# Identity products in the norms' waits, the output projection among retention's last sums, first values turned late

## Chip, cores and metric
One core of one Trainium2 chip. The metric is device microseconds of one execution; times of the kernel before are a median of three runs, and the profile is of a further execution.

## What is computed
Two layers on 512 latent tokens of width 1024 (and 256 context tokens). Layer 0 mixes with windowed attention beside retention, layer 1 with a Hyena long convolution; each layer has a half-step SwiGLU block before and after its mixer.

```python
def swiglu(h, w_gate, w_up, w_down):
    return (jax.nn.silu(h @ w_gate) * (h @ w_up)) @ w_down

def adaln_in(x, g, m, i):
    return rmsnorm(x, g) * (1.0 + m[:, :, 3 * i + 1]) + m[:, :, 3 * i]

def adaln_out(x, y, g, m, i, w):
    return x + w * m[:, :, 3 * i + 2] * rmsnorm(y, g)

# even layer: y = concat(window_attention, retention_out(o, g)) @ w_out
def retention_out(o, g):
    o = o * lax.rsqrt(jnp.mean(o * o, -1, keepdims=True) + EPS)
    return o.reshape(o.shape[0], o.shape[1], -1).astype(g.dtype) * jax.nn.silu(g)

# odd layer: y = (x0 * bidir_fftconv(v * x1)) @ w_out
```

All of it is float32; the kernel reaches that by splitting activations and weights into a high and a low part and adding three products.

## The kernel before
Activations lie with features on the partitions: eight tiles of 128 features by 512 tokens (256 for context). A weight block is 128 output features by 1024 inputs. SyncE loads it into one of four slots of `raw`; ScalarE copies it to `w_hi` (`split_hi`, L1159), VectorE writes the rest to `w_lo` (`split_lo`, L1698), and TensorE does `three` (L530) for each of its eight input tiles: 24 matmuls of 128x512 a block. Slots come round by the semaphores `lo_split` and `block_done`; results go to PSUM banks 0 to 3 in turn and are given back by `result_read`. Every engine has its program written out by hand in its own order, so an instruction that waits holds up all behind it on its engine.

**Fused norm.** Behind the output projection, two FFNs and the Hyena projection, the norm of the result and that of the next input are made together. `down` or `project` calls `early_sums` before the last six matmuls: three groups of four one-column sums (`stat`, L669), each two passes. `fused_norm` on TensorE (from L680) then waits for the last tile's square, sums it, sums `cross` and `gained`, waits for the reciprocal root (`norm_spread`, L718: four products of 128 columns with the identity), and again for `wide2` (L696, four more). VectorE makes x and `prod` tile by tile, ScalarE `h_hi`, VectorE `h_lo` (L1915), and the next gate/up or Hyena input takes four weight blocks side by side as the tiles come. In the order of time they are called A after the even mixer's projection, B and C after FFNs, and D after Hyena's projection.

**Mixer.** `mixer_second` goes through slots: `score`, a projection in parts (0 to 3, 3 to 6, 6 to 8 input tiles) with the turns of earlier probabilities between, then the probabilities times values. In slot 0 the first values are turned (L802) after part 0 to 3, once VectorE has copied them. `retention` ends with `sums(3)` (L1000) and `spread(3)` (L1006), each waiting for the other engines; `project` follows with eight blocks. Its inputs are attention tiles 0 to 3 and retention tiles 4 to 7, of which the last needs spread(3). In `project` VectorE does for each block: copy y (L2499), add the square, three gain sums, split a weight block two ahead; block 7 has two splits ahead of its copy.

**Hyena's end.** After the back transforms (L1107, L1110) TensorE waits until the gated tiles and the first projection weights are split.

Of the kernel before, what the change touches and what calls it, by code (L numbers as in the profile page):

```python
# [23 lines left out]
P = 128  # L24
# [125 lines left out]
def build(nc, io):  # L150
# [38 lines left out]
    with ExitStack() as ctx:  # L189
# [334 lines left out]
        def _(pe):  # L524
# [108 lines left out]
            def down(s, T, tiles, beside=lambda i: None, bank_of_sums=None):  # L633
# [4 lines left out]
                def step(i, last):  # L638
                    for dd in range(2):
# [4 lines left out]
                        for half in range(2):  # L644
# [3 lines left out]
                            d = 2 * i + dd  # L648
                            if bank_of_sums and half and d:
                                pe.wait_ge(square_ready, n0 + d)  # L650
                                stat(square[:, 1 - dd, :], T, d == 1, False, bank_of_sums).then_inc(square_used, 1)
                            for t in range(per):
                                f = half * per + t
                                if dd == 0 and (f == 0 or f == tiles - 1):

                                    pe.wait_ge(act_ready, f0 + (tiles - 1 if f == 0 else tiles))
                                if s.following and last and j == 3 and t == 3:
                                    early_sums(s)
                                ins = three(psum[:, bank, 0:T], (slot, t * P), P, act_hi[:, f, 0:T], act_lo[:, f, 0:T],
                                            f == 0, f == tiles - 1)  # L660
# [11 lines left out]

            def early_sums(s):

                sum2, sum3, _, _ = gain_buffers(s)
                pe.wait_ge(square_used, KT * at["norm"] + KT - 1)
                stat(sumsq, SEQ, True, False, STAT)
                pe.wait_ge(gain_sums, GAIN_OPS * at["fused"] + GAIN_OPS - 1)
                stat(sum2, SEQ, True, False, GAIN_STAT)
                stat(sum3, SEQ, False, False, GAIN_STAT, 4)  # L680

            def fused_norm(s):


                n, f = at["norm"], at["fused"]
                _, _, cross, gained = gain_buffers(s)
                pe.wait_ge(square_ready, KT * n + KT)
                stat(square[:, 1, :], SEQ, False, True, STAT).then_inc(square_used, 1)
                pe.wait_ge(gain_sums, GAIN_OPS * f + GAIN_OPS)
                stat(cross, SEQ, False, False, GAIN_STAT)  # L690
                pe.wait_ge(gained_ready, KT * f + KT)
                stat(gained[1], SEQ, False, True, GAIN_STAT, 4).then_inc(gain_summed, 1)
                norm_spread(SEQ)
                pe.wait_ge(wide2_ready, f + 1)
                for t in range(SEQ // P):
                    ins = pe.matmul(psum[:, RBC2, t * P:t * P + P], wide2[:, t, :], ident[:, :], start=True, stop=True)  # L696
                ins.then_inc(rbc2_ready, 1)
                at["fused"] += 1

# [27 lines left out]
            def ffn(ss, T):  # L727
# [5 lines left out]
                if ss[3].following:  # L733
                    fused_norm(ss[3])
                else:
                    norm(T, 1)

            def first_ffns():
# [11 lines left out]
                gate_up(sx[0], SEQ, ctx_norm, lambda: pe.wait_ge(filt_ready, PARTS))  # L750
                down(sx[1], SEQ, HALF_TILES[0])
                gate_up(sx[2], SEQ)
                down(sx[3], SEQ, HALF_TILES[1])
# [118 lines left out]
            def mixer_second():  # L872
# [37 lines left out]
                for s in range(len(SLOTS)):  # L910
                    if s >= 1:
                        score(s - 1)
                    proj(s, 0, 3)
                    if s == 0:
                        pe.wait_ge(v_copied, 1)
                        value_turn(lambda t: sumsq[:, t * P:t * P + P], 6, 4)
                        value_turn(lambda t: prod[:, 1, t * P:t * P + P], 7, 2).then_inc(v_turned, 1)
                    else:
                        if s >= 2:
                            turn(s - 2, 0)  # L920
                    proj(s, 3, 6)
                    if s >= 2:
                        turn(s - 2, 1)
                    proj(s, 6, KT)
                    if s >= 1:
# [4 lines left out]
            def retention():  # L930
# [107 lines left out]
                outputs(3)  # L1038
                spread(2)
                sums(3)  # L1040
                spread(3)

            def project(s, ready):

                for d in range(s.blocks):
                    b = s.first + d
                    pe.wait_ge(lo_split, RING + b + 1)
                    pe.wait_ge(result_read, at["p"] + 1)
                    for k in range(KT):
                        if d == 0:  # L1050
                            ready(k)
                        if d == KT - 1 and k == 6:
                            early_sums(s)
                        ins = three(psum[:, at["p"] % 4, :], (b % RING, k * P), P, h_hi[:, k, :], h_lo[:, k, :],
                                    k == 0, k == KT - 1)
# [5 lines left out]
            retention()  # L1061
            project(mix_out, lambda k: pe.wait_ge(att_out_ready, k + 1) if k < 4 else pe.wait_ge(ret_out_ready, k - 3))
            fused_norm(mix_out)
# [79 lines left out]
            pe.wait_ge(g_ready, KT // 2)  # L1143
            project(hy_out, lambda k: pe.wait_ge(g_split, k + 1))
            fused_norm(hy_out)
# [1638 lines left out]
```

## Time and profile before

| | |
|---|---|
| median of three runs | 2457.37 us (2457.02 to 2461.73) |
| the profiled execution | 2460.91 us |
| its span | 2459.2 us |
| TensorE busy | 2351.5 us, 96% |
| VectorE / ScalarE busy | 1368.3 us, 56% / 876.6 us, 36% |
| mean granted TensorE clock | 0.967 |
| DMA | 133 GB/s on average |

Busy shares are of the span. A matmul's time in a row is from its start to its modelled end; back to back they overlap, so prices are read from start to start. The clock of a stretch is the share of full speed that was granted.

### The profile page before, as it was taken

The page shows a single profiled execution, that of the slowest core. Times are in us where ns is not written, and L with a number is a line of the kernel's source. Part 1 is how long each engine was busy: PE and PEld are TensorE (multiplying, and loading weights), DVE is VectorE, ACT ScalarE, POOL GpSimd, SP SyncE. Part 2 cuts the span into 40 slices and gives each one's busy share as a digit, 9 for nine tenths or more (in the row PEclk, how much of TensorE's full clock was granted, in tenths as well). Part 3 has the DMA queues.
Part 4 walks back from the last instruction along what each step waited for, and adds up shares of the span by engine and source line. Part 5 has one row for each costly group of instructions (what it writes and reads, how often), then busy time and mean ns, then how long its engine had stood idle before and what let it go on. Part 6 is the DMA issues. An engine that isn't in the chain of part 4 may idle for free. (4 is left out here: it accounts for less than half of the span.)

```text
span 2459.2 us, 31552 instructions
## 1 busy us (share of the span) xinstructions
PE 2351.5 (96%) x11692; PEld 1933.6 (79%) x11692; DVE 1368.3 (56%) x2020; ACT 876.6 (36%) x1305; POOL 126.1 (5%) x245
## 2 busy tenths in 40 slices
PE   6999999999999988999999999999999989999997
PEld 2588788899987866788888788888877777888886
DVE  5677833575666564733367743743674587433334
ACT  1443122454544573433222432222354214322222
POOL 1022200000021000000011000200000000000000
PEclk8999999999999998899999899999999988999998
DMA  8578932345542101232367322842322212223222
GB/s 334 210 272 296 334 103 71 122 155 195 169 141 76 46 27 35 84 114 86 115 245 257 101 86 90 285 155 75 114 78 78 103 60 77 86 90 106 96 77 77
DMA packets 97104, 327.03 MB, mean 133 GB/s; under 512 B 12288, under 2 KB 12704, under 8 KB 95200
## 3 DMA queue, kind: packets, MB, share of 16 engines
q1 hardware_dynamic: 67968, 222.27, 26.6%
q0 software_dynamic: 28016, 101.99, 12.0%
q8 instruction: 73, 1.20, 0.2%
q10 hardware_dynamic: 1008, 1.25, 0.1%
q14 instruction: 39, 0.32, 0.0%
HBM read 313.67 MB, written 8.39 MB: 131 GB/s over the span
## 5 line engine op out<-in xcount | busy, mean ns | idle before, releaser
L533 PE MATMUL psum<-h_hi,w_hi 128*128 128x512 f32 (+1 forms) x2256 | 857.4, 380 | 28.9 <-DVE h_lo L1915 13.3
L534 PE MATMUL psum<-h_lo,w_hi 128*128 128x512 f32 (+1 forms) x2256 | 848.7, 376 | 0.0
L535 PE MATMUL psum<-h_hi,w_lo 128*128 128x512 f32 (+1 forms) x2256 | 848.2, 376 | 0.0
L1698 DVE TENSOR_TENSOR w_lo<-raw,w_hi 128x1024 fp32r<-128x1024 f32 (+2 forms) x442 | 470.8, 1101 | 87.7 <-ACT w_hi L1159 84.9
L533 PEld LDWEIGHTS psum<-h_hi,w_hi 128*128 128x128 f32 x2256 | 430.4, 191 | 112.4 <-issue 26.5
L1159 ACT ACTIVATE w_hi<-raw 128x1024 fp32r<-128x1024 f32 (+2 forms) x442 | 406.3, 951 | 245.5 <-PE psum L535 160.4
L535 PEld LDWEIGHTS psum<-h_hi,w_lo 128*128 128x128 f32 x2256 | 430.0, 191 | 77.0
L534 PEld LDWEIGHTS psum<-h_lo,w_hi 128*128 128x128 f32 x2256 | 430.6, 191 | 74.2 <-issue 0.7
L533 PE MATMUL psum<-act_hi,w_hi 128*128 128x512 f32 (+1 forms) x880 | 326.4, 371 | 4.9 <-DVE w_lo L1698 4.4
L535 PE MATMUL psum<-act_hi,w_lo 128*128 128x512 f32 (+1 forms) x880 | 324.7, 369 | 0.0
L534 PE MATMUL psum<-act_lo,w_hi 128*128 128x512 f32 (+1 forms) x880 | 324.6, 369 | 0.0
L1831 DVE TENSOR_TENSOR prod<-psum,square 128x512 f32<-128x512 f32 (+1 forms) x110 | 70.1, 638 | 432.5 <-PE psum L535 411.9
L1192 ACT ACTIVATE act_hi<-prod 128x512 f32 (+3 forms) x110 | 64.8, 589 | 506.2 <-DVE prod L1831 506.2
L533 PEld LDWEIGHTS psum<-act_hi,w_hi 128*128 128x128 f32 x880 | 166.6, 189 | 35.3 <-issue 6.3
L535 PEld LDWEIGHTS psum<-act_hi,w_lo 128*128 128x128 f32 x880 | 166.7, 189 | 27.7
L534 PEld LDWEIGHTS psum<-act_lo,w_hi 128*128 128x128 f32 x880 | 166.8, 190 | 27.1
L1732 DVE SCALAR_TENSOR_TENSOR mod_raw<-mod_raw,c_row 128x1024 f32<-128x1024 f32 x128 | 149.7, 1222 | 11.8 <-DMA mod_raw<-in_w_rows 10.4
L1190 ACT ACTIVATE square<-psum 128x512 f32<-128x512 f32 (+1 forms) x110 | 60.6, 551 | 191.9 <-PE psum L535 191.8
L2593 POOL DMA_DIRECT2D mod_raw<-in_w_rows x152 | 80.2, 528 | 804.6 <-DVE mod_raw L1732 718.3
L1836 DVE TENSOR_TENSOR act_lo<-prod,act_hi 128x512 f32 (+3 forms) x110 | 70.3, 639 | 91.1 <-ACT act_hi L1192 91.1
L1942 DVE COPY y<-psum 128x512 f32<-128x512 f32 (+3 forms) x40 | 25.5, 637 | 107.9 <-PE psum L535 107.8
L1245 ACT ACTIVATE square<-y 128x512 f32<-128x512 f32 (+2 forms) x40 | 23.4, 586 | 136.0 <-DVE y L1944 136.0
(298 smaller groups left out, 1778.4 us busy)
## 6 DMA issues: line engine op xcount, KB each, us to landing
raw<-in_gate_up SPq DMA_DIRECT2D x220, 512.0 KB, 4.2
mod_raw<-in_w_rows POOLq DMA_DIRECT2D x152, 512.0 KB, 5.5
raw<-in_down_a SPq DMA_DIRECT2D x80, 384.0 KB, 3.7
raw<-in_down_b SPq DMA_DIRECT2D x80, 320.0 KB, 3.1
raw<-in_hy_in SPq DMA_DIRECT2D x24, 512.0 KB, 3.4
raw<-in_mix_in SPq DMA_DIRECT2D x22, 512.0 KB, 4.1
mod_raw<-in_w_mod POOLq DMA_DIRECT2D x16, 512.0 KB, 7.1
filt_dram<-made SPq DMA_DIRECT2D x6, 1024.0 KB, 4.0
```

What stands on the lines that cost most here:

```text
L533: pe.matmul(out, w_hi[:, slot, c:c + P], hi, start=start, stop=False)
L534: pe.matmul(out, w_hi[:, slot, c:c + P], lo, start=False, stop=False)
L535: return pe.matmul(out, w_lo[:, slot, c:c + P], hi, start=False, stop=stop)
L1159: act.activation(w_hi[:, slot, 0:cols], raw[:, slot, 0:cols], ACT.Copy).then_inc(hi_split, 1)
L1190: act.activation(silu[:, j, 0:T], psum[:, bank, 0:T], ACT.Silu).then_inc(silu_ready, 1)
L1192: act.activation(act_hi[:, bass.ds(2 * i + j, 1), 0:T], prod[:, j:j + 1, 0:T], ACT.Copy).then_inc(act_hi_ready, 1)
L1698: ins = dve.tensor_tensor(w_lo[:, slot, 0:cols], raw[:, slot, 0:cols], w_hi[:, slot, 0:cols].bitcast(F32), ALU.subtract)
L1732: dve.scalar_tensor_tensor(src, src, 1.0, row, ALU.mult, ALU.mult, accum_out=mod_cols[:, k:k + 1]).then_inc(mod_used, 1)
L1831: ins = dve.tensor_tensor(prod[:, j, 0:T], psum[:, bank, 0:T], silu[:, j, 0:T], ALU.mult)
L1836: dve.tensor_tensor(act_lo[:, fl, 0:T], prod[:, j:j + 1, 0:T], act_hi[:, fl, 0:T].bitcast(F32), ALU.subtract).then_inc(act_ready, 1)
L1942: dve.tensor_copy(dst, src).then_inc(result_read, 1)
L2593: pool.dma_start(mod_raw[:, k % RING, :], src).then_inc(mod_landed[k % RING], 16)
```

## The change
A helper `keep_busy(n)` issues n products of the identity with itself (128 columns, into the PSUM bank that comes next) and waits at most for that bank to be read. It is called in all fused norms (3, 2, 1, 6 and 13 products), before the last norm (5), before the second gate/up of the first FFN (8), before the last square's sums of the context FFN (8) and before Hyena's output projection (13). `early_sums` is cut into three groups, before input tile 6, before 7, and after the last matmul. In slot 0 the values are turned after all input tiles. The first two blocks of the output projection are done in `retention`: six tiles of block 0 after spread(2), two of block 1 after sums(3), the rest after spread(3).

```diff
@@ down
                             if bank_of_sums and half and d:
+                                if d == KT - 1:
+                                    keep_busy(8)
                                 pe.wait_ge(square_ready, n0 + d)
...
-                                if s.following and last and j == 3 and t == 3:
-                                    early_sums(s)
+                                if s.following and last and j == 3 and t >= 3:
+                                    early_sums(s, t - 3)
@@
+            def keep_busy(n):
+
+                pe.wait_ge(result_read, at["p"] + 1)
+                for _ in range(n):
+                    pe.matmul(psum[:, at["p"] % 4, 0:P], ident[:, :], ident[:, :], start=True, stop=True)
+
+            def early_sums(s, part):
 
                 sum2, sum3, _, _ = gain_buffers(s)
+                if part == 0:
+                    pe.wait_ge(square_used, KT * at["norm"] + KT - 1)
+                    stat(sumsq, SEQ, True, False, STAT)
+                elif part == 1:
+                    pe.wait_ge(gain_sums, GAIN_OPS * at["fused"] + GAIN_OPS - 1)
+                    stat(sum2, SEQ, True, False, GAIN_STAT)
+                else:
+                    stat(sum3, SEQ, False, False, GAIN_STAT, 4)
@@ fused_norm
+                early_sums(s, 2)
+                keep_busy(3)
                 pe.wait_ge(square_ready, KT * n + KT)
                 stat(square[:, 1, :], SEQ, False, True, STAT).then_inc(square_used, 1)
+                keep_busy(2)
                 pe.wait_ge(gain_sums, GAIN_OPS * f + GAIN_OPS)
                 stat(cross, SEQ, False, False, GAIN_STAT)
+                keep_busy(1)
                 pe.wait_ge(gained_ready, KT * f + KT)
                 stat(gained[1], SEQ, False, True, GAIN_STAT, 4).then_inc(gain_summed, 1)
                 norm_spread(SEQ)
+                keep_busy(6)
                 pe.wait_ge(wide2_ready, f + 1)
...
                 ins.then_inc(rbc2_ready, 1)
+                keep_busy(13)
                 at["fused"] += 1
@@ ffn
+                    keep_busy(5)
                     norm(T, 1)
@@ first_ffns
                 down(sx[1], SEQ, HALF_TILES[0])
+                keep_busy(8)
                 gate_up(sx[2], SEQ)
@@ mixer_second
                     proj(s, 0, 3)
+                    if s >= 2:
+                        turn(s - 2, 0)
+                    proj(s, 3, 6)
+                    if s >= 2:
+                        turn(s - 2, 1)
+                    proj(s, 6, KT)
                     if s == 0:
                         pe.wait_ge(v_copied, 1)
                         value_turn(lambda t: sumsq[:, t * P:t * P + P], 6, 4)
                         value_turn(lambda t: prod[:, 1, t * P:t * P + P], 7, 2).then_inc(v_turned, 1)
...
@@ retention
                 spread(2)
+                out_part(0, range(6))
                 sums(3)
+                out_part(1, range(2))
                 spread(3)
...
+                out_part(1, range(2, 6))
+                out_part(0, range(6, 8))
+                out_part(1, range(6, 8))
+                at["p"] += 2
+
+            def out_part(d, tiles):
+
+                b, p = mix_out.first + d, at["p"] + d
+                pe.wait_ge(lo_split, RING + b + 1)
+                pe.wait_ge(result_read, p + 1)
+                for k in tiles:
+                    if k >= 4:
+                        pe.wait_ge(ret_out_ready, k - 3)
+                    ins = three(psum[:, p % 4, :], (b % RING, k * P), P, h_hi[:, k, :], h_lo[:, k, :], k == 0, k == KT - 1)
+                if KT - 1 in tiles:
+                    ins.then_inc(block_done, 1)
@@
-            project(mix_out, lambda k: pe.wait_ge(att_out_ready, k + 1) if k < 4 else pe.wait_ge(ret_out_ready, k - 3))
+            project(mix_out, 2)
             fused_norm(mix_out)
@@ after hyena
             pe.wait_ge(g_ready, KT // 2)
-            project(hy_out, lambda k: pe.wait_ge(g_split, k + 1))
+            keep_busy(13)
+            project(hy_out, 0, lambda k: pe.wait_ge(g_split, k + 1))
```

## Rows read from the trace of the kernel before

**Rows 1.** The page, part 2: granted TensorE clock in 40 slices, in tenths.
```profile
PEclk8999999999999998899999899999999988999998
```

**Rows 2.** Windows: length, TensorE busy (matmuls), granted clock, DMA share, GB/s.
```profile
924.50:931.50 7.00, 7.00 (x90) 1.00 0.01 2
1009.90:1025.20 15.30, 9.30 (x41) 0.50 0.20 66
1025.30:1030.00 4.70, 4.70 (x11) 0.50 0.00 0
1100.00:1150.00 50.00, 50.00 (x222) 1.00 0.27 84
1394.90:1408.80 13.90, 9.24 (x34) 0.52 0.12 38
1771.00:1791.20 20.20, 14.10 (x52) 0.50 0.21 76
2069.50:2084.80 15.30, 10.64 (x45) 0.56 0.11 35
```

**Rows 3.** Timeline, TensorE in norm A: start, us, engine, line, [idle before <-releaser].
```profile
1011.37 1.87 PE L669 MATMUL psum<-ones,square 128*128 128x1 f32 x8 [1.45 <-ACT square L1611]
1013.10 3.55 PE L669 MATMUL psum<-ones,spare_post 128*128 128x1 f32 x16
1016.51 2.05 PE L718 MATMUL psum<-ident,full 128*128 128x128 f32 x8
1019.89 2.07 PE L696 MATMUL psum<-ident,full 128*128 128x128 f32 x8 [1.33 <-DVE full L1892]
1025.30 0.77 PE L533 MATMUL psum<-h_hi,w_hi 128*128 128x512 f32 x1 [3.33 <-DVE h_lo L1915]
```

**Rows 4.** Timeline, norms B and C: first early sums and first block matmul after.
```profile
1387.38 0.95 PE L669 MATMUL psum<-ones,sumsq 128*128 128x1 f32 x8
...
1404.83 0.77 PE L533 MATMUL psum<-h_hi,w_hi 128*128 128x512 f32 x1 [3.33 <-DVE h_lo L1915]
...
1767.58 0.95 PE L669 MATMUL psum<-ones,sumsq 128*128 128x1 f32 x8
...
1787.87 0.77 PE L533 MATMUL psum<-h_hi,w_hi 128*128 128x512 f32 x1 [3.33 <-DVE h_lo L1915]
```

**Rows 5.** Timeline, TensorE at the end of retention: spread(2), sums(3), spread(3).
```profile
951.78 1.16 PE L1006 MATMUL psum<-ident,full 128*128 128x128 f32 x8
957.01 1.87 PE L1000 MATMUL psum<-head_ones,full 128*128 128x2 f32 x8 [4.07 <-ACT full L1543]
959.94 2.07 PE L1006 MATMUL psum<-ident,full 128*128 128x128 f32 x8 [1.06 <-DVE full L2441]
```

**Rows 6.** Timeline, VectorE's copies of blocks 0, 1, 3, 7 in the output projection.
```profile
969.15 0.69 DVE L2499 COPY y<-psum 128x512 f32<-128x512 f32 x1 [2.23 <-PE psum L535]
...
974.59 0.69 DVE L2499 COPY y<-psum 128x512 f32<-128x512 f32 x1 [1.26 <-PE psum L535]
...
985.47 0.69 DVE L2499 COPY y<-psum 128x512 f32<-128x512 f32 x1 [0.30 <-PE psum L535]
...
1009.97 0.69 DVE L2499 COPY y<-psum 128x512 f32<-128x512 f32 x1 [1.90 <-PE psum L535]
```

**Rows 7.** Timeline: the first values' turn on TensorE, the first scores' reading on VectorE.
```profile
749.12 0.66 PE L802 MATMUL psum<-ident,sumsq 128*128 128x128 f32 x4 [3.25 <-DVEq L2264]
...
756.68 0.69 DVE L2297 TENSOR_SCALAR probs<-psum 128x512 f32<-128x512 f32 x1
```

**Rows 8.** Timeline, TensorE's four other waits that get products, or stand behind them.
```profile
302.52 0.47 PE L533 MATMUL psum<-h_hi,w_hi 128*128 128x512 f32 x1 [2.32 <-DVE w_lo L1698]
...
675.26 0.98 PE L669 MATMUL psum<-ones,square 128*128 128x1 f32 x4 [2.21 <-ACT square L1245]
...
2018.13 0.77 PE L533 MATMUL psum<-h_hi,w_hi 128*128 128x512 f32 x1 [3.61 <-issue]
...
2443.13 1.05 PE L669 MATMUL psum<-ones,square 128*128 128x1 f32 x8 [0.66 <-ACT square L1245]
```

More of the change, by code:

```diff
@@ L671, in stat @@
                 return ins
-            def early_sums(s):
-                sum2, sum3, _, _ = gain_buffers(s)
[L676 to L680, printed above, removed]
+            def keep_busy(n):
[3 more added lines that the diff above has]
+            def early_sums(s, part):
+                sum2, sum3, _, _ = gain_buffers(s)
+                if part == 0:
[6 more added lines that the diff above has]
+                    stat(sum3, SEQ, False, False, GAIN_STAT, 4)
             def fused_norm(s):
@@ L917, in mixer_second @@
                         value_turn(lambda t: prod[:, 1, t * P:t * P + P], 7, 2).then_inc(v_turned, 1)
[L918 to L924, printed above, removed]
                     if s >= 1:
@@ L1039, in retention, with project @@
                 spread(2)
+                out_part(0, range(6))
                 sums(3)
+                out_part(1, range(2))
                 spread(3)
-            def project(s, ready):
-                for d in range(s.blocks):
+                out_part(1, range(2, 6))
[12 more added lines that the diff above has]
+                    ins.then_inc(block_done, 1)
+            def project(s, d0=0, ready=None):
+                for d in range(d0, s.blocks):
                     b = s.first + d
@@ L1049, in project @@
                     for k in range(KT):
-                        if d == 0:
+                        if ready and d == 0:
                             ready(k)
-                        if d == KT - 1 and k == 6:
-                            early_sums(s)
+                        if d == KT - 1 and k >= 6:
+                            early_sums(s, k - 6)
                         ins = three(psum[:, at["p"] % 4, :], (b % RING, k * P), P, h_hi[:, k, :], h_lo[:, k, :],
```

## The prediction
> **What bounds the kernel now.** I read the page first. TensorE is busy in 96% of the span, so only two things can be won: time in which it waits, and time in which it works at the lower clock. The clock line [rows 1] shows where: it stands at 9 in most slices and dips in a few. I then put windows over those dips [rows 2]. In 1009.90:1025.20 the granted clock is 0.50, in 1025.30:1030.00 still 0.50 though TensorE works without a pause (11 matmuls in 4.70 us, 0.427 each), and in an undisturbed stretch it is 1.00 (222 in 50.00 us, 0.225 each). These are the two levels, 1.2 and 2.4 GHz. So a norm costs three times: the wait itself, its own small matmuls at half speed, and the first block matmuls after it at half speed. The timeline of the norm after the mixer [rows 3] gives its links; two FFN norms follow [rows 4], then the end of retention [rows 5], VectorE in the output projection [rows 6], the first values [rows 7] and four single waits [rows 8].
>
> **Prices.** An identity product is one f32 matmul of 128 columns in two passes. Four of them take 1.16 us at the full clock [rows 5], 1.09 without the tail, so 0.27 each; at the low clock 2.05 to 2.07 [rows 3, 5], 1.72 without the tail, 0.43 each. A group of four one-column sums takes 0.95 at full clock (0.9 start to start) [rows 4], and 1.73 from the first to the next at half clock [rows 3].
>
> **A fused norm, clock held.** Counted from the start of the square's sums: sums 0.9, two products 0.54, cross sums 0.9, one product 0.27, gained sums 0.9, so the first spread starts at 3.5. It takes 1.09. The second spread needs the first one's result plus a VectorE multiply, reciprocal and copy: before, it started 3.38 after the first (1016.51 to 1019.89), with 2.05 of that in the first spread at half clock, so 1.3 remain after its end: it could start at 6.05. The six products end at 3.5+1.09+1.63 = 6.2, so it starts 0.2 late. It ends at 7.3. From its end to the first matmul there is a wait of 3.33 [rows 3]; thirteen products take 3.54. First matmul: 10.9. Before, it was 1025.30-1011.37 = 13.93. In front of the square's sums the third group of sums moves behind the last matmul, into a wait of 1.45 [rows 3] plus the matmul's tail, together 1.6; with three products it takes 0.9+0.82 = 1.7. The groups before it keep their price. From the first sums to the first matmul the new path is 0.9+0.68+0.9+0.68+1.7+10.9 = 15.7.
> - B (FFN): 1404.83-1387.38 = 17.45 becomes 15.7; and the clock stays up after it (4.0 us at half clock until 1408.80 [rows 2], 2.0 lost): 3.8 gained.
> - C (FFN): 1787.87-1767.58 = 20.29, 4.6 plus 1.7 for 1787.87 to 1791.20: 6.3.
> - D (after Hyena): only its windows row stands here; its mean clock of 0.56 is as late a fall as B's: 3.8.
> - A (after the mixer), from the square's sums: 13.93-10.9 = 3.0, plus 2.2 for the 11 slow matmuls (4.70-11*0.225): 5.2.
>
> **Clock not quite held.** Between the last block matmul and the first spread stand four groups of one-column sums (3.6 us) and six products (1.6), so columns run less than a third of that time. In 924.50:931.50 a stretch of 128-column matmuls without a pause stayed at 1.00 [rows 2], but all four norms fell in or just after their sums. I take the likeliest case to be one fall in the middle of each norm, with the six and thirteen products bringing the clock back before the block matmuls. Then two groups of sums (0.8 more each) and a part of the products are slow: 2.0 per norm. Ends: 0 (held) and everything slow (second rival). This leaves A 3.2, B 1.8, C 4.3, D 1.8: 11.1 together.
>
> **Output projection among retention's last sums.** Before: spread(2) 951.78 to 952.87, then a wait of 4.07 for ScalarE's square, sums 957.01, a wait of 1.06, spread(3) 959.94, and block 0 from 961.66 [rows 5] at half clock. Now 18 matmuls (4.05) fill the first wait to 956.9, so the sums start when they did; 6 fill the second; spread(3) ends at 960.4 at full clock; 24 more end at 965.8. The last ret_out tile is ready 2.8 after the spread, 963.3, and is wanted at 963.8. Before, both blocks ended at 961.66+48*0.225+1.8 = 974.2. TensorE is 8.4 earlier, but VectorE is next. Its copy of block 0 stood at 969.15 after an idle 2.23 [rows 6]; its work ahead of that hangs on the spread and moves 1.6 earlier, so the copy can start at 965.3. Up to the copy of block 7 it is 40.82 us, of which idle 1.26+5*0.30+1.90 = 4.66 [rows 6]. With no idle at all it reaches it at 1001.5, 8.5 earlier. The price of this step is therefore limited by VectorE, and the sums ahead of the last matmuls now wait for VectorE's block 6; I take 8.3. Lower bound 3.8 (only what block 0's copy gains), upper 8.5. Weights of both blocks are split well before (the splits run two ahead), so nothing is queued on them.
>
> **First values late.** TensorE waited 3.25 for the copies after 9 matmuls [rows 7] and then did 15 more. Now all 24 stand ahead of the wait, ending at 749.1 as the copies land; the first scores could start that wait earlier, and a little more if the clock stays up, 3.9 at most. But VectorE reads them at 756.68 [rows 7], behind the sixteen-column logarithm chain, not behind TensorE; so the next scores, which wait for the reading, gain 1.9. Bounds 0 and 3.9.
>
> **Single waits [rows 8].** Before the second gate/up: eight products (2.18) in a wait of 2.32 for w_lo; if the clock stays up, the slow start behind it goes, taken as long as C's (3.3 us, 1.7 lost): 1.7, lower bound 0. Last context block: eight in 2.21 before sums that took 0.98 for four passes, twice the full-clock price; with them (0.4) and the 15 matmuls of 256 columns behind them (0.1 less each) 1.9, lower bound 0. Hyena's end: thirteen (3.54) in 3.61, then, at 0.77 for the first matmul as after the norms, a slow start like A's, with the copies behind it: 2.6, between 2.0 and 2.8. Final norm: five products (1.36) stand ahead of sums that ran in a wait of which only 0.66 was left; the clock was high anyway, so this costs 0.7. SP's queue is not touched; the weight loads follow VectorE's splits, which come earlier. GpSimd's modulation loads after x_ready move with the norm.
>
> **Sum.** 11.1 + 8.3 + 1.9 + 1.7 + 1.9 + 2.6 - 0.7 = 26.8. The profiled execution took 2460.91 (span 2459.2), so it would be 2434.1; the three timed runs have the median 2457.37, 3.5 lower, and I forecast against that: 2430.6.
>
> **A rule against it.** In 924.50:931.50, where nothing but matmuls of 128 columns runs, an identity spread among them, the clock was 1.00 [rows 2]. The Trainium skill, "TensorE: Matmul & The Clock Gate", Part 4, says that transposes through TensorE do not count as work for the clock as matmuls do. The products here take an identity but are issued as plain matmuls, and that stretch agrees with them counting. Were they not to count, the rival below called slower would hold.
>
> **Rivals.**
> - *Held throughout.* All four norms keep 1.00; 4*2.0 more: 2422.6. For it: 924.50:931.50. Against: the sums' share above. Chance 0.17.
> - *Low through the norms.* The fall comes early and the clock is back only after the restart; moving sums and covering waits just balance, the norms give nothing, and only the rest remains: 26.8-11.1 = 15.7, 2441.7. Chance 0.16.
> - *No change.* As the next one in the norms, but clock held at the other three places: -18.6-0.7+8.3+1.9+1.7+1.9+2.6 = -2.9, 2460. Chance 0.04.
> - *Slower.* Products do not hold or raise the clock anywhere, and being in order they delay what follows. Per norm at 0.43: three behind a slow sum (1.73+1.29 against 1.6) 1.4, two and one 1.3, six 2.6 against 1.65 0.9, thirteen 5.6 against 3.7 1.9; less 0.9 for the moved sum: 4.6, four times 18.6. Hyena 2.0, final 0.7, less 8.3 and 1.9: 11 slower, 2468. It decides where the clock is still at 0.50 when the six products end. Chance 0.04.
> - *Forecast,* with parts off by their bounds: 0.59, own range 2425 to 2437.
>
> Time can be told from no change beyond about 0.2% (4.9 us). Faster 0.92, same 0.04, slower 0.04. The range 2421 to 2443 takes in held and low-through-the-norms.
>
> **What would show it.** Right: in each norm the first h matmul about 11 us after the square's sums, at 0.39 long and not 0.63; the first matmuls after Hyena at 0.39; the copy of block 7 near 1001 less the earlier gains (5.7), with VectorE idle before it under 0.5. Wrong: rows of 0.43 per product across the thirteen; a wait in front of out_part for a weight; first scores still read more than 10 us after the values' turn; sums in the final norm not delayed.

## Result and the profile after

| | before | after |
|---|---|---|
| median | 2459.55 us (4 runs, 2457.02 to 2463.89) | 2434.2 us (4 runs, 2428.19 to 2436.48) |
| profiled execution, its span | 2460.91, 2459.2 | 2433.61, 2431.9 |
| mean granted TensorE clock | 0.967 | 0.983 |

The ratio is 0.9897, with a 95% interval of 0.9875 to 0.9919: 1.0% faster. The forecast was 2434.1 for the profiled execution and 2430.6 for the median. Against its own before the median fell by 25.4; 26.8 was forecast.

**The clock.** The clock line of the page after, against [rows 1]: five of the six dips behind the first slice are gone, and the one that is left, in slice 16, lies at the end of the mixer.
```profile
PEclk8999999999999998999999999999999999999999
```
Windows of the kernel after (length, TensorE busy (matmuls), granted clock, DMA share, GB/s), against [rows 2]: the low stretches of norms A, B, C and D, and between them what follows A.
```profile
999.90:1006.70 6.80, 6.80 (x34) 0.50 0.24 80
1006.80:1010.70 3.90, 3.53 (x32) 1.00 0.00 0
1010.80:1015.50 4.70, 4.70 (x21) 1.00 0.00 0
1378.80:1382.20 3.40, 3.40 (x18) 0.50 0.52 154
1754.40:1761.10 6.70, 6.70 (x33) 0.50 0.24 78
2044.50:2051.20 6.70, 6.70 (x32) 0.50 0.25 78
```
In each norm the clock still falls once, for 3.4 to 6.7 us where it was 13.9 to 20.2 before. After that it is back: 4.70 us behind norm A take 21 block matmuls, not 11.

**Norm A.** Timeline of TensorE after (start, us, engine, line, [idle before <-releaser]), against [rows 3]; L679 is the products, L735 the first spread, L712 the second.
```profile
995.59 0.95 PE L671 MATMUL psum<-ones,spare_post 128*128 128x1 f32 x8
996.39 0.91 PE L679 MATMUL psum<-ident 128*128 128x128 f32 x6
997.43 1.05 PE L671 MATMUL psum<-ones,square 128*128 128x1 f32 x8
...
1000.04 1.71 PE L671 MATMUL psum<-ones,spare_post 128*128 128x1 f32 x8
1001.62 2.05 PE L735 MATMUL psum<-ident,full 128*128 128x128 f32 x8
1003.46 2.77 PE L679 MATMUL psum<-ident 128*128 128x128 f32 x12
1006.02 1.40 PE L712 MATMUL psum<-ident,full 128*128 128x128 f32 x8
1007.26 3.07 PE L679 MATMUL psum<-ident 128*128 128x128 f32 x26
1010.76 0.47 PE L533 MATMUL psum<-h_hi,w_hi 128*128 128x512 f32 x1 [0.43 <-DVE h_lo L1952]
```
The fall comes in the last sums (1.71 and not 0.95). The first spread and the six products are slow (2.77 for twelve passes), and they hold the second spread up by 1.0: it starts 4.40 after the first, against 3.38 in [rows 3]. The thirteen are fast (3.07 for 26 passes). The first block matmul comes 13.33 after the square's sums; a held norm was counted at 10.9, one fall at 2.0 more. "Held" is said below of a norm in which the clock does not fall.

**Output projection.** The end of retention after, against [rows 5]: spread(2), block 0, sums(3), spread(3), and VectorE's copies of blocks 0 and 7, against [rows 6].
```profile
947.01 1.16 PE L1024 MATMUL psum<-ident,full 128*128 128x128 f32 x8
947.92 0.48 PE L533 MATMUL psum<-h_hi,w_hi 128*128 128x512 f32 x1
...
952.24 1.05 PE L1018 MATMUL psum<-head_ones,full 128*128 128x2 f32 x8
...
954.61 1.05 PE L1024 MATMUL psum<-ident,full 128*128 128x128 f32 x8
...
960.49 0.68 DVE L2536 COPY y<-psum 128x512 f32<-128x512 f32 x1
...
996.03 0.68 DVE L2536 COPY y<-psum 128x512 f32<-128x512 f32 x1
```
sums(3) starts 5.23 after spread(2), as before (5.23). No copy has an idle time in front of it. From spread(2) to the copy of block 0 it is 13.48, before 17.37: 3.89 gained, 3.85 counted. From there to block 7 it is 35.54, before 40.82.

**Where the time went, site by site.** VectorE's 2020 instructions stand in the same order in both kernels and in all those below. So the start of one and the same instruction can be subtracted, and the difference of two such shifts is what a stretch gained. The table is worked out so from the traces, in us against the kernel after (positive: the other kernel is slower there); "predicted" is the prediction's term. Norm A begins at the copy of block 6, so it holds the early sums in block 7. Each column rests on one execution.

| stretch | predicted | before | no products | sums together | norms only |
|---|---|---|---|---|---|
| second gate/up | 1.7 | 2.3 | 0.7 | 0.4 | 0.2 |
| last context FFN | 1.9 | 0.4 | 0.3 | 0.0 | -0.1 |
| first values | 1.9 | 0.3 | 0.0 | 0.1 | 1.4 |
| retention's end, blocks 0 to 6 | 8.3 | 8.6 | 0.0 | 1.5 | 8.7 |
| norm A | 3.2 | 4.9 | 0.5 | 2.2 | -1.9 |
| norm B | 1.8 | 3.0 | 2.1 | 2.5 | 0.0 |
| norm C | 4.3 | 3.8 | 0.5 | 3.4 | 0.0 |
| Hyena's end | 2.6 | 2.6 | 2.7 | 0.0 | 2.8 |
| norm D | 1.8 | 1.3 | 2.1 | 0.9 | -1.6 |
| final norm | -0.7 | -0.3 | -0.1 | 0.0 | -0.3 |
| all other stretches | 0 | 0.4 | 3.7 | 2.9 | 2.0 |
| whole | 26.8 | 27.3 | 12.3 | 13.8 | 11.2 |

The last row but one is not the change's. It is made up mostly of the arrival of weights in the context part (from -2.0 to 1.2), a fall of the clock at the context norm or none (1.5 or 0), and a late modulation load between norms B and C (up to 4.0).

### The profile page after: what moved, and what is told of

It reads as the page before. It is cut to its first block and busy times, and to the rows that moved or that the text cites. A ratio compares the mean times of both kernels' runs of the same rounds, so it can differ in the third digit from the quotient of the medians.

```text
span 2431.9 us, 32091 instructions
## 1 busy us (share of the span) xinstructions
PE 2355.9 (97%) x11960; PEld 1946.8 (80%) x11960; DVE 1367.6 (56%) x2020; ACT 876.3 (36%) x1305; POOL 126.1 (5%) x245
## 3 DMA queue, kind: packets, MB, share of 16 engines
q0 software_dynamic: 28016, 101.99, 12.2%
```

## Experiments

**The kernel after once more.**

> The changed kernel itself, once more, beside the kernels of this group on their chip. Expected 2430 to 2436, and each norm again with one low stretch of 3.4 to 6.8 us. What differs between this trace and the first one of the same kernel is the play of one execution: arrival of weights in the context part, and where a fall of the clock lands. It gives the size below which a site's shift says nothing.

2432.16 us, ratio 0.9892 (0.9874 to 0.9911). Some kernels below were measured beside it on the same chip; for them this is "the kernel after of its group". All stretches of the table agree with the first trace within 0.12 us but three: the start of the context part (1.3 faster), the stretch between B and C (2.95 slower), and norm C, 3.0 faster. There the clock did not fall at all:
```profile
1748.50:1764.00 15.50, 15.09 (x123) 1.00 0.41 137
```
So one and the same norm is held or not from one execution to the next, and a fall in its middle for 6.7 us costs 3.0. From the start of the last block matmul to that of the next stage's first it is 12.17 held and 15.17 fallen. Over five executions of four kernels that have both the split sums and the identity products (this one, the norms' part alone, output projection as before, values as before), 20 norms: 3 took 12.2, 6 took 13.5 to 13.6 (a fall of 3.4 us), 11 took 15.2 to 15.4.

**No products.** `keep_busy` does nothing.
```diff
             def keep_busy(n):
-                pe.wait_ge(result_read, at["p"] + 1)
-                for _ in range(n):
-                    pe.matmul(psum[:, at["p"] % 4, 0:P], ident[:, :], ident[:, :], start=True, stop=True)
+                pass
```

> The changed kernel without any identity product; the order of the sums, the early output blocks and the late values stay. Forecast theory (the products bring the clock back before each restart): their share is 11.1 (norms) + 1.7 + 1.9 + 2.6 - 0.7 = 16.6 us by the prediction; by the shifts in the changed kernel's trace it is nearer 12 to 14. So 12 to 17 us above the changed kernel's 2434.2: 2446 to 2451, ratio 0.995 to 0.997 to the kernel before, with the clock at 0.50 again through the norms and the first block matmuls behind them, those at the 0.63 step and not 0.39. The 8.3 to 9.2 us of the output projection stay. Rival (the reordering of the sums and the earlier blocks made the gain, and the products only filled idle time): within 4 us of 2434, the norms as short as with products.

2444.63 us, ratio 0.9947 (0.993 to 0.9965), 10.4 above 2434.2 (12.3 by the ratios, each against its own before), the low end of the expected 12 to 17. Norm A of this kernel:
```profile
998.32 1.05 PE L671 MATMUL psum<-ones,square 128*128 128x1 f32 x8 [0.89 <-ACT square L1646]
999.24 2.19 PE L671 MATMUL psum<-ones,spare_post 128*128 128x1 f32 x16
1001.29 2.05 PE L733 MATMUL psum<-ident,full 128*128 128x128 f32 x8
1004.67 2.07 PE L710 MATMUL psum<-ident,full 128*128 128x128 f32 x8 [1.33 <-DVE full L1927]
1010.08 0.77 PE L533 MATMUL psum<-h_hi,w_hi 128*128 128x512 f32 x1 [3.33 <-DVE h_lo L1950]
```
The forecast theory holds in kind: the restart is slow again (0.77). Its size falls. By the traces the whole is 12.3, but 3.7 of it lie elsewhere; at the products' sites it is 8.7, not 16.6, and in the norms 5.1. The square's sums to the first block matmul are 11.76, shorter than the 13.33 with products: those delay the norm by 1.6, and what they return is the restart. In A and C that leaves 0.5, in B and D 2.1.

**Early sums side by side,** all products kept.
```diff
-                                if s.following and last and j == 3 and t >= 3:
-                                    early_sums(s, t - 3)
+                                if s.following and last and j == 3 and t == 3:
+                                    for part in range(3):
+                                        early_sums(s, part)
...
-                early_sums(s, 2)
                 keep_busy(3)
```

> The changed kernel with the three early groups of sums side by side before the last six matmuls, as before the change; all products stay. By the prediction's count the third group then costs 0.9 at full clock on the path in each norm, and the wait it filled is idle but for three products: 3 to 4 us above the changed kernel. Taking the traces apart (kernel before against the one without products) gave the order of the sums 2.4, 0.9, 3.3 and -0.8 in the four norms, 5.9 together: then 6 above. Rival (the split is worth nothing, a sum more or less before the square only shifts the wait for ScalarE): within 1.5.

2443.16 us, ratio 0.993 (0.9914 to 0.9946): 11.0 above the kernel after of the same group. By the traces it is 13.8, of which 8.9 lie in the norms. Norm A of this kernel:
```profile
999.78 1.42 PE L672 MATMUL psum<-ones,spare_post 128*128 128x1 f32 x6
1003.76 1.48 PE L680 MATMUL psum<-ident 128*128 128x128 f32 x6
1005.41 1.32 PE L672 MATMUL psum<-ones,square 128*128 128x1 f32 x8 [0.16 <-ACT square L1649]
```
In norm A the clock falls in these sums, ahead of the last six block matmuls, which then run slow, and so do the three products behind them (1.48 against 0.91). There TensorE also waits 0.69 for VectorE between the first group and the second. In norm C it falls during those six block matmuls, in B and D not before the later sums. Both expectations were too low. Splitting the sums was counted at 0.9 per norm, the time of one group. In D, where the clock falls once with either order, it is 0.87, just that. The mean is 2.2, so some 5.4 of the 8.9 come through the clock and, in A, that wait, by one execution of each kernel.

**The norms' part alone,** on the kernel before.

> The kernel before with the fused norms' part of the change alone: sums in three groups and the products 3, 2, 1, 6 and 13; no products elsewhere, output projection and values as before. Prediction: 11.1 us below the kernel before, between 0 (clock low to the restart) and 19 (held in all four). By the shifts in the changed kernel's trace 11.0 (2.9, 3.0, 3.8, 1.3). From a median of 2457 to 2459 before: 2446 to 2448, ratio 0.9955. Each norm that shows 12.2 from its last block matmul to the next stage's first was held, each of 15.2 fell in the middle.

2443.85 us, ratio 0.9945 (0.9929 to 0.9961), 12.8 below the kernel before of its group, against 11.1. In norm A the clock was held here (12.18), in B and D it fell for 3.4 us (13.5 each), in C for 6.7 (15.17). By the traces these four norms are 16.4 below those of the kernel before, 3.5 more than in the kernel after, so this execution was a lucky one.

**Without 3, 2 and 1.**
```diff
-                keep_busy(3)
...
-                keep_busy(2)
...
-                keep_busy(1)
```

> The changed kernel without the 3, 2 and 1 products between the sums; the six and the thirteen stay. If the early six only stand in the way (the clock falls among the sums with or without them), each norm is up to 1.3 us shorter, 1.6 at most: 3 to 6 us below the changed kernel. If they push the fall back or shorten it, it comes sooner and takes the square's sums, both spreads and a part of the block matmuls: 2 to 6 us above. Forecast theory as written leans to the first only where the thirteen still bring the clock back before the first block matmul; low stretches of 6.8 or less then, of 10 or more otherwise.

2436.79 us, ratio 0.9902 (0.9881 to 0.9923), 4.6 above the kernel after of its group. By the traces the norms lose 0.7, 2.5, -0.7 and 0.9, together 3.4, and the low stretches are 6.8 to 10.2 long. So the six early products do more than stand in the way, if not in every norm.

**Wide products.** One pass of 512 columns each, of the input tile that is no longer needed.
```diff
+            def keep_wide(n):
+                pe.wait_ge(result_read, at["p"] + 1)
+                for _ in range(n):
+                    pe.matmul(psum[:, at["p"] % 4, :], h_hi[:, 0, 0:P], h_hi[:, 1, :], start=True, stop=True)
...
-                keep_busy(3)
+                keep_wide(3)
...
-                keep_busy(2)
+                keep_wide(4)
...
-                keep_busy(1)
+                keep_wide(3)
```

> The changed kernel with 3, 4 and 3 one-pass products of 128x512 (the old input tile with itself, 0.225 us each) in place of 3, 2 and 1 two-pass identity products of 128 columns between the sums; six and thirteen stay. They put 5120 columns among the sums for 1536 and take 2.25 us for 1.6. Where a norm is held, its path from the square's sums to the first block matmul is 10.33 (seen once, in norm A of the kernel without early blocks) plus 0.9 for more products behind that start; with one fall it was 13.33. Theory (more columns keep the clock at full through the sums): no low stretch in the norms, 2 to 3 us gained in each less 0.65: 5 to 9 us below the changed kernel, 2424 to 2429. Rival (it is the number of matmuls or the waits, not columns, and the clock falls all the same): 2.6 us or more above it.

2428.74 us, ratio 0.9874 (0.9856 to 0.9892), 3.4 below the kernel after of its group, where 5 to 9 were expected. B, C and D were held (13.12, three times), but A fell: 16.34. B had been short already, so the gain against the kernel after is 0.4, 2.05 and 2.05 in B, C, D, and A loses 0.9. One thing that set A apart is seen in its rows.
```profile
997.54 0.94 PE L685 MATMUL psum<-h_hi 128*128 128x512 f32 x3
998.57 1.05 PE L671 MATMUL psum<-ones,square 128*128 128x1 f32 x8
```
The start of the square's sums lies 1.03 behind that of the three products (0.80 in norm C). Around its early sums A has 0.1 more too. Whether this brought the clock down, or only the play of one execution, is not shown.

**Four wide products each time.**

> The changed kernel with 4, 4 and 4 one-pass products of 128x512 between the sums in place of 3, 2 and 1 identity products. With 3, 4 and 3 the norms B, C and D had no low stretch and took 13.12 from the last block matmul to the first one of the next stage (15.17 where one fall lay in the middle, 12.17 where a norm with identity products was held by luck); norm A fell and took 16.34. Theory (columns among the sums decide): two more products (0.45) hold A as well: all four norms at 13.6, A 2.7 shorter than with 3, 4, 3, the others 0.45 longer, so about 1.3 below that kernel's 2428.7: 2426 to 2429. Rival (A falls for another reason, the mixer's tail ahead of it): A again over 16, and 1.8 above it.

2429.98 us, ratio 0.9887 (0.9868 to 0.9906). All four norms held: 13.58, 13.46, 13.46, 13.46, which is 1.8, 0.1, 1.7 and 1.7 below the first trace of the kernel after. The rival's 16 in norm A did not come. The median is not below 2428.74, where 1.3 less was expected; the sum of 5.3 is near what medians can tell (their intervals are some 4.6 us to each side), and a final norm that was 0.8 longer in this execution took a part of it. The price of the wider products, in norm A of this kernel:
```profile
999.90 1.17 PE L685 MATMUL psum<-h_hi 128*128 128x512 f32 x4
1000.90 0.95 PE L671 MATMUL psum<-ones,spare_post 128*128 128x1 f32 x8
```
Four take 1.00 from start to start, twelve 3.0; the six narrow ones took 1.6. The wide ones thus bring more columns and more time between the sums, and no kernel had narrow ones for 3.0 us. So it is not shown which of the two holds the clock.

**Combined:** wide products 4, 4 and 4, no five before the last norm, and output blocks spread over one wait more.
```diff
+                out_part(0, range(4))
                 sums(2)
                 outputs(3)
                 spread(2)
-                out_part(0, range(6))
+                out_part(0, range(4, 6))
+                out_part(1, range(4))
                 sums(3)
-                out_part(1, range(2))
+                out_part(1, range(4, 6))
                 spread(3)
-                out_part(1, range(2, 6))
                 out_part(0, range(6, 8))
                 out_part(1, range(6, 8))
```

> The kernel with 4, 4 and 4 wide products, without the five before the last norm, and with four input tiles of output block 0 (12 matmuls, 2.7 us of work that is wanted anyway) in TensorE's wait of 2.61 before the sums of retention's third pair; block 0's tiles 4 and 5 and block 1's tiles 0 to 3 then fill the wait behind spread(2). Expected: that wait is covered and the clock doesn't fall at its place, where outputs(3) began at half clock (two of its four chunks at 1.67 and not 0.95): 1.5 to 2 us. VectorE sets the pace up to block 7, so the 12 matmuls taken off behind the last spread give nothing more. The five products less: 0.3 to 0.8. Together 2 to 3 us below the kernel with wide products 4, 4, 4: 2423 to 2427, 1 to 1.5% below the kernel before. Rival (block 1's weights are split too late, TensorE waits for w_lo ahead of the last sums): that gain is lost and retention ends 1 to 3 us later.

2426.44 us, ratio 0.9881 (0.9862 to 0.99). Windows of this kernel over norms A to D:
```profile
986.50:1010.00 23.50, 23.06 (x150) 1.00 0.27 90
1363.00:1385.00 22.00, 21.57 (x146) 1.00 0.28 96
1740.00:1762.00 22.00, 21.57 (x146) 1.00 0.28 96
2026.00:2048.00 22.00, 21.57 (x146) 1.00 0.27 91
```
Retention's end gains 1.4, a little under what was counted for outputs(3) at the full clock. TensorE now waits 2.19 for the last input tile:
```profile
955.08 0.49 PE L533 MATMUL psum<-h_hi,w_hi 128*128 128x512 f32 x1 [2.19 <-DVE h_lo L2498]
```
Leaving the five out gave little: the final norm was 0.4 longer than in the kernel after, where they stand, and 0.4 shorter than in the kernel with four wide products, where they stand too.

> The combined kernel once more, on whatever chip, to see whether its four held norms are a property of the order or of one execution. If 4, 4 and 4 wide products hold the clock wherever the norm lies: again 13.5 to 13.6 from the last block matmul to the next stage's first in all four, and 2423 to 2429. If it was luck, as with the identity products (the second FFN norm once 15.17 and once 12.17 with one and the same kernel), at least one norm shows 15 to 16.5.

2429.25 us, ratio 0.9883 (0.9867 to 0.99). The norms took 13.46, 13.46, 13.47 and 13.47, so with four wide products twelve norms out of twelve were held, in three executions. Behind the wait of 2.19 for the last input tile, though, the clock fell in this execution (0.50 in 956.40:959.60), as it did not in the first: such a wait is not always free. The ratios of this kernel (0.9881, 0.9883) lie below those of the kernel after (0.9897, 0.9892), but the intervals overlap, and the lowest ratio of all is that of 3, 4 and 3 (0.9874). That the norms are shorter than in the kernel after is told by the traces' stretches; which of the kernels with wide products is fastest is not shown.

**Output projection as before.**
```diff
-                out_part(0, range(6))
                 sums(3)
-                out_part(1, range(2))
                 spread(3)
...
-            project(mix_out, 2)
+            project(mix_out, 0, lambda k: pe.wait_ge(att_out_ready, k + 1) if k < 4 else pe.wait_ge(ret_out_ready, k - 3))
```

> The changed kernel with all eight output blocks behind retention as before; products, sums and values as changed. Theory (TensorE fills two waits, and VectorE then sets the pace to block 7): 8 to 9.2 us above 2434.2, so 2442 to 2444, with VectorE's copies of y idle again before blocks 0, 1 and 7, and its copy of block 7 8 to 9 us later against the last copy of the mixer. Rival (only what block 0's copy gains, 3.8): 2438. Rival (the gain was given back at norm A, because the last squares hang on VectorE anyway): the copy of block 7 later, but the first matmul after the norm not.

2439.85 us, ratio 0.9931 (0.9916 to 0.9946), 5.7 above 2434.2 and 7.7 above the kernel after's second median; by the ratios, each against its own before, it is 8.4 and 9.6. Up to block 6 it loses 8.6, as do the kernel before and the norms alone (8.6, 8.7): the best reproduced number of this study. Then 1.9 come back by the end of norm A, which was held in this execution, with 10.33 from the square's sums to the first block matmul:
```profile
1008.05 1.05 PE L671 MATMUL psum<-ones,square 128*128 128x1 f32 x8
...
1012.39 1.50 PE L679 MATMUL psum<-ident 128*128 128x128 f32 x12
1013.89 1.16 PE L712 MATMUL psum<-ident,full 128*128 128x128 f32 x8
1014.88 3.07 PE L679 MATMUL psum<-ident 128*128 128x128 f32 x26
1018.38 0.47 PE L533 MATMUL psum<-h_hi,w_hi 128*128 128x512 f32 x1 [0.43 <-DVE h_lo L1946]
```
The third theory (given back at norm A) is right for 1.9. It may be more than chance. Norm A was held in both kernels without the early blocks (12.17 here, 12.18 with the norms' part alone) and fell in the three executions with them and the same products (15.4). With them VectorE's copy of block 7 waits for VectorE's own work, the last square comes later, and the square's sums start 2.08 after the last block matmul, not 1.84. Whether these 0.24 bring the clock down was not tried by itself.

**Values as before.**
```diff
                     proj(s, 0, 3)
+                    if s == 0:
+                        pe.wait_ge(v_copied, 1)
+                        value_turn(lambda t: sumsq[:, t * P:t * P + P], 6, 4)
+                        value_turn(lambda t: prod[:, 1, t * P:t * P + P], 7, 2).then_inc(v_turned, 1)
...
-                    if s == 0:
-                        pe.wait_ge(v_copied, 1)
...
```

> The changed kernel with slot 0's values turned after input tiles 0 to 3 as before. Prediction: 1.9 us above 2434.2 (bounds 0 and 3.9). By the changed kernel's trace only some 0.3 us was kept, because the time came back as a wait at the second slot's scores; then within 1 us, which a time can't tell from none: it is to be read from the trace, as the distance between an instruction ahead of the turn and the one some slots behind it. Expected: a wait of about 3 us before the turn, waits at the scores shorter by 1.3 to 3 us, and the distance over the slots the same within 0.5 us.

2432.5 us, ratio 0.9895 (0.9878 to 0.9913): no change that a time can tell. From the values to the output blocks the shifts are 1.4 in the slots, then -2.4 and 1.3 in retention, together 0.3. In retention the clock fell at other places than in the kernel after (0.50 in 918.50:921.70 and 939.00:945.60, against 914.70:921.30, 931.80:935.00 and 942.00:945.20), and the kernel with the norms' part alone, where the values are early too, shows 1.4 without those shifts. So I take 1.4 as what the values give. Rows of the kernel after: TensorE's turn, its scores of the next slot, the first turn of probabilities, and a window between the last two:
```profile
745.96 0.66 PE L821 MATMUL psum<-ident,sumsq 128*128 128x128 f32 x4
756.69 0.92 PE L860 MATMUL psum<-ak,aq 64*128 64x384 f32 x4 [2.01 <-DVE stats L2343]
761.73 0.60 PE L874 MATMUL psum<-ident,probs 128*128 128x128 f32 x4
757.60:761.00 3.40, 3.40 (x18) 0.50 0.45 154
```
and the same in the kernel with the values early:
```profile
759.21 0.92 PE L860 MATMUL psum<-ak,aq 64*128 64x384 f32 x4
762.74 0.60 PE L874 MATMUL psum<-ident,probs 128*128 128x128 f32 x4
759.20:762.70 3.50, 3.50 (x27) 1.00 0.38 147
```
The wait before the turn is gone, and 2.01 of waiting for VectorE stand before the next scores. In the kernel after they start 2.5 earlier all the same. But behind the new wait the clock falls: from the scores to the turn of probabilities it is 5.04 us, with the values early 3.53. So 1.5 of the gain go to the clock, in the first 5 us behind it.

**Transposes in place of products,** `for _ in range(2 * n): pe.transpose(...)` of the identity.

> The changed kernel with each two-pass identity product replaced by two transposes of the identity through TensorE, one pass each, so the same number of passes of 128 columns. If such transposes don't count as work for the clock (the Trainium skill, TensorE: Matmul & The Clock Gate, Part 4), the clock is at 0.50 through the norms and into the restart, and what they cost on the way is added: 12 to 28 us above 2434.2, that is 2446 to 2462. If they count as the products do: 2430 to 2438, clock back up before the first block matmul in every norm. Passes per transpose would be near 0.12 us at the full clock and 0.22 at half, as those of the products.

2431.64 us, ratio 0.9903 (0.9885 to 0.992). Norm A of this kernel:
```profile
1001.00 2.77 PE L679 MATMUL psum<-ident 128*128 128x128 f32 x12
1003.56 1.56 PE L712 MATMUL psum<-ident,full 128*128 128x128 f32 x8
1004.96 3.00 PE L679 MATMUL psum<-ident 128*128 128x128 f32 x26
```
Twelve slow transposes take 2.77 as the twelve slow passes did, 26 fast ones 3.00 against 3.07, and from the last block matmul to the next stage's first it is 15.3, 13.4, 13.4 and 15.1, each some 0.1 below a value that norms with products showed. On these rows they do for the clock what the products do. The Trainium skill, "TensorE: Matmul & The Clock Gate", Part 4, says that transposes don't count as TensorE's being busy in the same way; these rows don't agree, for f32 transposes of the identity as this kernel issues them. The trace calls them MATMUL, so it does not show in which mode of the engine they ran.

## Why the prediction was right, point by point

- **Bound and prices.** Right. A product is 0.24 inside a long row (3.07 for 13), counted 0.27.
- **Norms, 11.1.** 12.9 by the table. The picture was right: one fall in the middle, the clock back before the restart. The first block matmul came 13.33 after the square's sums in three norms and 11.70 in B, not the "about 11" of the sign. Two sizes were off. A fall in the middle costs 3.0, not the 2.0 of "Clock not quite held". Start to start, norm A's slow links against those of a held norm are one group of sums (1.58, held 0.81), the first spread (1.84, 0.97), the six products (2.56, 1.50) and the second spread (1.24, 0.99); two groups of sums and a part of the products had been counted. Against it stands the split of the sums, which the prediction priced at the 0.9 of one group that leaves the path: it gives 7.8 by the kernel before less the one without products, over the four norms, and 8.9 by the kernel with the sums together. The products give 5.1. So by these traces the larger part of the norms' gain came from the step to which the prediction gave the smaller.
- **Output projection, 8.3.** 8.6 up to block 6, and 9.2 from spread(2) to block 7 (17.37+40.82 less 13.48+35.54), above the upper bound of 8.5. That bound took off the idle time in front of the copies alone (4.66 of the 5.28). The other 0.6 is that a copy without a wait starts 0.08 before the recorded end of the instruction ahead of it, seven times. The wait of 0.76 before the adding of a square is there in both kernels. In both kernels without the early blocks 1.9 of the 8.6 come back by the end of norm A.
- **First values, 1.9.** 0.3 against the kernel before, 1.4 against each of two other kernels with the values early (norms only, values as before); the turn itself ran at the full clock in the first (0.66 in [rows 7]) and at the low one in these (1.11). The shift is 3.2 at the values and 3.1 at the first scores' reading (756.68 in [rows 7], 753.58 after), so VectorE did not move there, as predicted. The next scores did gain their 1.9: 1.83 (761.68 before, 756.69 after, less the 3.16 that was gained ahead of it). The step that failed is taking this gain as kept. TensorE now waits 2.01 ahead of them, the clock falls behind that wait, and 1.5 are lost.
- **Second gate/up, 1.7.** 2.3 against the kernel before, but 0.2 to 0.7 against kernels in which the clock didn't fall there without products either. The term is right only for executions with that fall.
- **Last context FFN, 1.9.** 0.4. It was gained and given back: behind the sums VectorE's shift is 1.9 larger, and 16 us later 1.56 of it is gone. The faster TensorE comes to a wait for VectorE, and the clock falls behind it, where in the kernel before it stayed up. First the kernel after, then a window of the kernel before:
```profile
681.50 0.49 PE L533 MATMUL psum<-h_hi,w_hi 128*128 128x512 f32 x1 [1.79 <-DVE h_lo L2035]
682.60:685.80 3.20, 3.20 (x9) 0.50 0.77 216
```
```profile
682.10:690.00 7.90, 7.32 (x34) 1.00 0.81 256
```
From this matmul to the four identity matmuls of the context norm it is 8.31 us, before 6.74: the 1.56. The prediction left out this price of a moved wait, here and at the values.
- **Hyena's end, 2.6.** 2.6, and 2.7 and 2.8 by two kernels without its products.
- **Final norm, -0.7.** -0.3. The five products take 1.11 from their start to that of the sums:
```profile
2413.93 1.28 PE L679 MATMUL psum<-ident 128*128 128x128 f32 x10
2415.04 0.95 PE L671 MATMUL psum<-ones,sumsq 128*128 128x1 f32 x8
```
- **Rivals.** Held throughout came true in 3 of 20 norms; low through the norms and slower in none. What spoke for the first, the full clock in 924.50:931.50, was weak: the clock of the kernel before is 0.50 in 917.60:924.20 and again in 934.70:937.90. The rule on transposes, on which the last stood, was not borne out by the transposes tried here.

The misses of the terms that fell short (values, context FFN: 3.1) and of those that exceeded (norms, output projection, second gate/up, final norm: 3.1) cancel. The other stretches made 0.4 more. That the sum was met to 0.5 us in the profiled executions is therefore partly luck, the more so as one norm alone varies by 3.0.

## What to carry over

Where TensorE must wait or do thin work, look at the order of that work, not only at idle time: three groups of one-column sums side by side cost more through the clock than through their length, and splitting them was worth more than the products put between. Fillers that take the place of a wait cost nothing; those between links of a chain cost their own length, and at half clock nearly twice that. Twelve one-pass products of 512 columns (3.0 us) held twelve norms of twelve, six narrow ones (1.6 us) three of twenty; narrow ones for 3.0 us were not tried. A gain at one wait must be followed to the next wait of the same engine before it is counted, and the clock behind that wait too. Two of the seven terms lost most of their gain so, within 16 us (1.5 of 1.8 and 1.6 of 2.0): each time TensorE came early to a wait of 1.8 to 2.0 us, and the clock fell behind it for 3.4 us.

## What was not expected of the hardware

- The same kernel in two executions showed one norm at 12.17 and at 15.17: whether a thin stretch brings the clock down depends on more than the program, so a single trace prices such an edit only to about 3 us a place.
- Transposes of the identity kept the clock as plain products did (15.3, 13.4, 13.4, 15.1 against 15.4, 13.5, 15.2, 15.2).
- With 3, 4 and 3 wide products the clock fell in norm A and not in C, though their rows differ by little: 0.2 more in front of the square's sums and 0.1 around the early sums. That this was the cause was not tried by itself.
